# Two hybrid transformer layers on one core: input sums of the MLP made in halves, and two weight sums of the first down projection on GpSimd

## The reference

```python
for l in range(DEPTH):                              # DEPTH = 2
    h = rms_norm(x, norm_mix[l])
    proj = h @ w_in[l]                              # 1024 -> 1792
    ...
    x = x + jnp.concatenate([att, sgu], axis=-1) @ w_o[l]
    h = rms_norm(x, norm_ffn[l])
    x = x + jnp.square(jax.nn.relu(h @ w_up[l])) @ w_down[l]   # 1024 -> 4096 -> 1024
return rms_norm(x, norm_final)
```

## Time and profile before

| | |
|---|---|
| median of 3 executions | 950.86 us (948.45 to 953.03) |
| profiled execution | 949.33 us |
| its span on the core | 947.4 us |
| TensorE matmul busy (PE) | 930.3 us, 98% |
| VectorE busy (DVE) | 707.8 us, 75% |
| ScalarE busy (ACT) | 563.8 us, 60% |
| GpSimd busy (POOL) | 204.8 us, 22% |

### The profile page before, as it was taken

One profiled execution on the slowest core, in us unless ns is written; L12 is line 12 of the kernel. 1 busy time (PEld: TensorE's weight loads), 2 busy tenths in 40 slices (PEclk: granted clock), 3 DMA queues, 4 the chain that ended last, 5 costly groups with the idle time before them and its releaser, 6 DMA issues.

```text
span 947.4 us, 14055 instructions
## 1 busy us (share of the span) xinstructions
PE 930.3 (98%) x5632; PEld 819.0 (86%) x5632; DVE 707.8 (75%) x813; ACT 563.8 (60%) x843; POOL 204.8 (22%) x136
## 2 busy tenths in 40 slices
PE   8999999989999999999999999999899999999997
PEld 5888889978998998899888887899689989989985
DVE  5685525999779869879948752478987897798697
ACT  5556517775576376457655574377645756754764
POOL 2554224110011101011146433240101101101010
PEclk9999999999999999999999999999999999999999
DMA  9442150677668676676543320518668666676772
GB/s 292 127 135 71 42 150 28 167 166 206 147 171 204 134 232 134 178 190 156 165 150 134 112 68 23 155 24 245 139 173 205 149 198 158 161 198 150 205 156 89
DMA packets 40497, 141.76 MB, mean 150 GB/s; under 512 B 5616, under 2 KB 5744, under 8 KB 40432
## 3 DMA queue, kind: packets, MB, share of 16 engines
q1 hardware_dynamic: 28624, 98.32, 30.9%
q0 software_dynamic: 11520, 41.95, 25.3%
q10 hardware_dynamic: 288, 0.59, 0.2%
HBM read 138.74 MB, written 2.10 MB: 149 GB/s over the span
## 4 chain that ended last, share of the span: by engine, by line
PE 89%; DVE 6%; DMA 2%; ACT 1%; issue 1%; POOL 0%; DVEq 0%
PE bank L578 15%; PE bank L579 14%; PE bank L580 14%; PE bank L581 13%; PE bank L583 13%; PE bank L582 13%; DVE wlo L1316 2%; DMA raw<-weights_in 2%; PE bank L605 1%; PE bank L833 1%; PE bank L781 1%; DVE raw L1593 1%; PE bank L816 1%; PE bank L826 1%; PE bank L807 1%
## 5 line engine op out<-in xcount | busy, mean ns | idle before, releaser
L938 ACT ACTIVATE whi<-raw 128x1024 fp32r<-128x1024 f32 x268 | 281.0, 1057 | 165.2 <-PE bank L580 81.2
L1316 DVE TENSOR_TENSOR wlo<-raw,whi 128x1024 fp32r<-128x1024 f32 x218 | 264.8, 1223 | 79.8 <-ACT whi L938 79.4
L581 PE MATMUL bank<-xhi,wlo 128*128 128x256 f32 (+1 forms) x672 | 208.8, 311 | 0.0
L583 PE MATMUL bank<-xlo,whi 128*128 128x256 f32 (+1 forms) x672 | 207.3, 309 | 0.0
L582 PE MATMUL bank<-xhi,whi 128*128 128x256 f32 (+1 forms) x672 | 207.2, 308 | 0.0
L578 PE MATMUL bank<-wlo,fhi 128*128 128x512 f32 x448 | 176.3, 393 | 7.8 <-DVE flo L1580 7.8
L550 POOL DMA_DIRECT2D raw<-weights_in x80 | 69.4, 868 | 509.8 <-DVE raw L1593 236.0
L537 POOL TENSOR_TENSOR wlo<-raw,whi 128x1024 fp32r<-128x1024 f32 x50 | 135.2, 2714 | 195.4 <-ACT whi L938 195.4
L579 PE MATMUL bank<-whi,fhi 128*128 128x512 f32 x448 | 175.8, 392 | 0.0
L580 PE MATMUL bank<-whi,flo 128*128 128x512 f32 x448 | 175.5, 392 | 0.0
L581 PEld LDWEIGHTS bank<-xhi,wlo 128*128 128x128 f32 x672 | 128.3, 191 | 6.8 <-issue 0.3
(11 more groups left out here) (131 smaller groups left out, 1240.7 us busy)
## 6 DMA issues: line engine op xcount, KB each, us to landing
raw<-weights_in SPq DMA_DIRECT2D x172, 512.0 KB, 4.3
raw<-weights_in POOLq DMA_DIRECT2D x80, 512.0 KB, 6.1
xt<-x_in SPq DMA_DIRECT2D x4, 512.0 KB, 8.3
gbc<-gains_in SPq DMA_DIRECT2D x4, 512.0 KB, 4.3
out_t<-xt SPq DMA_DIRECT2D x3, 512.0 KB, 2.6
gbc<-gains_in ACTq DMA_DIRECT2D x1, 512.0 KB, 5.8
bias<-alibi_in SPq DMA_DIRECT2D x2, 256.0 KB, 7.3
wst<-ws_in SPq DMA_DIRECT2D x2, 256.0 KB, 7.0
```

What stands on the lines that cost most here:

```text
L581: pe.matmul(o, wlo[:, s, wc], hi[:, tokens], start=first, stop=False, skip_group_check=on_sum)
L583: return pe.matmul(o, whi[:, s, wc], lo[:, tokens], start=False, stop=last, skip_group_check=on_sum)
L938: act.activation(whi[:, n % SLOTS, :], raw_at(slot), ACT.Copy).then_inc(whi_ready, 1)
L1316: dve.tensor_tensor(wlo[:, n % SLOTS, :], raw_at(raw_slot(n)), whi[:, n % SLOTS, :], ALU.subtract) \
```

## The change

Three edits, all in the MLP of each layer.

1. `xs_make(i)` becomes `xs_make(i, k)`: k = 0 makes the sum for tokens 0 to 127 of each block, k = 1 for the other 128. The halves k = 0 are made inside the norm's last tile, xs_make(0, 0) ahead of its reciprocal and the other three behind its normalisation; the halves k = 1 stand where the whole sums stood. `xs_made` counts eight in place of four, and `xs_high` waits for the half k = 1.
2. In quarter 0, `sum_m6(l, q, g)` for the down projection is done by GpSimd, between its DMAs for M7 and those for M5; VectorE has it no more there.
3. In quarter 0, `make(q, 0)` stands between the low halves of M1's two blocks, one place earlier.

```diff
+def made_x(l, i, k):
+
+    return l * 8 + 4 * k + i + 1
...
+            def sum_m6(l, q, g):
+
+                wait_low(pool, nth(l, group_pos(q, DOWN, M7, g)))
+                pool.wait_ge(raw_landed[PRODUCT_SLOT[DOWN][M1] + g], 16 * block_loads(l, q, DOWN, M1, g))
+                t3 = raw_at(PRODUCT_SLOT[DOWN][M7] + g)
+                pool.tensor_tensor(t3, t3, raw_at(PRODUCT_SLOT[DOWN][M1] + g), ALU.add).then_inc(weights_summed, 1)
...
                     add_blocks(l, q, DOWN, M7)
+                    if q == 0:
+                        sum_m6(l, q, 0)
+                        sum_m6(l, q, 1)
                     add_blocks(l, q, DOWN, M5)
...
+                def xs_make(i, k):
+
+                    x11, x12, x22, x21 = (xf[:, b, :, tok(k)] for b in range(4))
+                    if i == 0:
+                        dve.wait_ge(xf_ready, l * 2 * NT + 6 + 2 * k)
+                        dve.tensor_tensor(s3[:, :, tok(k)], x11, x21, ALU.subtract).then_inc(xs_made, 1)
...
                 for t in range(NT):
                     add(1, t)
                     if t:
                         turned_low(2 * l + 1, t - 1)
+                    if t == NT - 1:
+                        xs_make(0, 0)
                     normed(2 * l + 1, t)
+                for i in range(1, 4):
+                    xs_make(i, 0)
                 turned_low(2 * l + 1, NT - 1)
...
                         low_down(q, M1, 0)
+                        make(q, 0)
                         low_down(q, M1, 1)
...
                     low_down(q, M7, 0)
-                    sum_m6(q, DOWN, 0)
+                    if q:
+                        sum_m6(q, DOWN, 0)
                     factor_low(q, M7)
                     low_down(q, M7, 1)
-                    sum_m6(q, DOWN, 1)
+                    if q:
+                        sum_m6(q, DOWN, 1)
                     low_down(q, M6, 0)
```

More of the change, by code:

```diff
@@ L1139, in xs_high @@
                 def xs_high(i):
-                    made, src = ((1, s3), (3, xf[:, 0, :, :]), (2, xf[:, 3, :, :]), (4, xf[:, 1, :, :]))[i]
-                    act.wait_ge(xs_made, l * 4 + made)
+                    made, src = ((0, s3), (2, xf[:, 0, :, :]), (1, xf[:, 3, :, :]), (3, xf[:, 1, :, :]))[i]
+                    act.wait_ge(xs_made, made_x(l, made, 1))
                     act.copy(factor_x((S3, S2, S5, S4)[i])[0], src).then_inc(xs_hi, 1)
@@ L1514, in add @@
                         .then_inc(x_added, 1)
+                def xs_make(i, k):
[3 more added lines that the diff above has]
+                        dve.tensor_tensor(s3[:, :, tok(k)], x11, x21, ALU.subtract).then_inc(xs_made, 1)
+                    elif i == 1:
+                        dve.wait_ge(xs_made, made_x(l, 0, k))
+                        dve.tensor_tensor(x21, x22, x21, ALU.subtract).then_inc(xs_made, 1)
+                    elif i == 2:
+                        dve.wait_ge(xs_made, made_x(l, 1, k))
+                        dve.scalar_tensor_tensor(x11, x21, -1.0, x11, ALU.mult, ALU.subtract).then_inc(xs_made, 1)
+                    else:
+                        dve.wait_ge(xs_made, made_x(l, 2, k))
+                        dve.scalar_tensor_tensor(x12, x11, -1.0, x12, ALU.mult, ALU.subtract).then_inc(xs_made, 1)
                 for t in range(NT):
@@ L1621, in _ @@
                     if q == 0:
-                        xs_make(0)
+                        xs_make(0, 1)
                         low_up(q, M7, 0)
@@ L1626, in _ @@
                         low_up(q, M7, 1)
-                        xs_make(1)
-                        xs_make(2)
+                        xs_make(1, 1)
+                        xs_make(2, 1)
                         low_up(q, M6, 0)
@@ L1640, in _ @@
                         low_up(q, M5, 0)
-                        xs_make(3)
+                        xs_make(3, 1)
                         up_sum(q, M4, 0)
@@ L1677, in _ @@
                         up_sum(q, M5, 1)
-                    make(q, 0)
+                        make(q, 0)
                     low_down(q, M7, 0)
-                    sum_m6(q, DOWN, 0)
+                    if q:
+                        sum_m6(q, DOWN, 0)
                     factor_low(q, M7)
                     low_down(q, M7, 1)
-                    sum_m6(q, DOWN, 1)
+                    if q:
+                        sum_m6(q, DOWN, 1)
                     low_down(q, M6, 0)
```

## The result

| | before | after |
|---|---|---|
| median | 951.05 us (6 executions, 948.45 to 953.03) | 963.28 us (6 executions, 961.85 to 965.96) |
| ratio | | 1.0129, 95% interval 1.0109 to 1.0149 |
| span of the profiled execution | 947.4 us | 961.3 us |

The change makes the kernel 12.2 us slower. The forecast was 956.4 us, which is 5.5 us slower, and a range to 963.0. The sign was right, the loss is more than twice the forecast, and the time is just outside the range. The two profiled executions lie 13.9 us apart; the one before took 949.33 us, 1.7 under its median.

The account below looks back on a forecast made before the run. TensorE, busy 98% of the span, was taken as the bound. A layer: +1.0 - 0.25 + 2.0 = +2.75, two layers +5.5 us, on the median 950.86 giving 956.4; range 952.5 to 963.

Parts of the forecast that it names:

- The prices that were taken from held instructions in the mixer: Earlier rows: held VectorE multiplies end 0.55 us (128x512) or 1.09 us (128x1024) after GpSimd; held GpSimd 2.26 after VectorE.
- I take it that VectorE wins: Norm's last tile: GpSimd asks 0.04 us before the normalisation, yet VectorE goes first; TensorE stands 0.75 us.
- the first rival: GpSimd wins at the norm's last tile, TensorE stands 3.0 us; 960.4 us, 964 with slow clock; chance 0.28.
- The row that I leaned on: VectorE's second multiply began within 0.01 us of GpSimd's 51.74; GpSimd was held, 2.94 us.
- The forecast's term of +1.0 us a layer: Norm to M6's second up low half: late VectorE makes TensorE 1.0 us later than before.
- +2.0 - 0.25 a layer: Quarter 0 down projection: M6's factor 2.0 us later through holding by GpSimd's sums, less 0.25 from the fourth sum.
- The late half of the fourth sum: At 184.75, saves between nothing and 0.54 us of what follows; 0.25 taken.
- The moved make: make(q, 0) moves into VectorE's 0.94 us of idleness in quarter 0's down projection and costs nothing.
- M4's adding DMA: Quarter 0 down: issued behind GpSimd's sum 2, its low half ends by 220.4, TensorE wants it at 221.7; covered by 1.3 us.
- if the wait at M6 shrinks: Sign that the forecast is wrong; it expected TensorE's waits at M6 about 1.3 us longer each.
- four rows of holding, not five: The prediction cited five rows all showing holding against its third rival, that GpSimd's sum doesn't hold VectorE, chance 0.10.

Follow-up runs that it names:

- e5: Kernel before plus a VectorE subtraction with two SBUF inputs (128x512) ahead of the norm's last reciprocal; 957.56 us, 1.0072 of the kernel before.
- e6: Kernel before plus a VectorE reduction with one SBUF input, same place and columns; 951.14 us, 1.0004 of the kernel before.
- e2: Kernel before with only the quarter 0 weight sums for M6 moved to GpSimd; 956.63 us, 1.0056 of the kernel before.
- e7: e2 with three GpSimd zero fills in place of each add, M6 left out of both quarter 0 down projections; 952.95 us, 1.0017 of the kernel before.
- e4: Changed kernel plus one small ScalarE square root in the norm's last tile, so GpSimd asks later; 958.29 us, 1.0079 of the kernel before.
- e3: Kernel before with only make(q, 0) moved one place earlier in quarter 0; 950.39 us, 0.9994 of the kernel before.
- e1: Kernel before with only the halved input sums; 957.18 us, 1.0059 of the kernel before.
- e10: Kernel before with, in quarter 0, make 0 earlier, both hidden(M5) before M1's second copy, M6's factor before its second block's low half; 946.39 us, 0.9958.

## Why the prediction was right or wrong

**Right: the mechanism and the sign.** VectorE and GpSimd hold each other up when VectorE's instruction has two SBUF inputs and GpSimd's reads SBUF. e5 against e6 shows the first condition, e2 against e7 the second. The prices that were taken from held instructions in the mixer came out within 0.05 us: the first half 1.61 (1.64 by the sum, 157.76 to 159.40), M7's factor 2.64 (2.66), make 1 3.39 (3.43), the second sum 3.28 (3.32).

**Wrong: the step "I take it that VectorE wins".** GpSimd won in both layers, by 0.01 us in the first (159.43 to 159.44) and 0.04 in the second. That was the first rival, with 0.28 against 0.40 for the forecast. The row that I leaned on has both starting at 51.74 us. It tells nothing of a case in which GpSimd is ahead, and my own times had it ahead, by 0.04 us. The forecast's term of +1.0 us a layer became +2.8, as the rival's 3.0 had it. When GpSimd is made to ask later (e4), the term is +0.96. So the arithmetic of both branches held, and the choice between them failed.

**Wrong: the clock left out at that place.** It fell in one of the two layers, 2.7 us more, and the forecast's sum had no term for it. The rival's text had it, at 1.8 us for each layer, and the range ended below it. With both branches joined, 9.5 + 1.8 to 2.7, the first rival gives 962.2 to 963.1, and the measured 963.28 is that case. That it comes within a microsecond is partly luck, since what the clock takes differs between executions (last section).

**Right: the down projection.** The forecast was +2.0 - 0.25 a layer; measured +3.16 and +1.25. Most of the scatter is the load of M1's second block, which is issued when VectorE has made the low half of M5's second, and which VectorE's chain waits for. Before, in the first layer, the end of that low half and the start of ScalarE's copy of the loaded block were 187.71 and 195.97, 8.26 us apart:

```profile
186.49 1.22 DVE L1316 TENSOR_TENSOR wlo<-raw,whi 128x1024 fp32r<-128x1024 f32 x1
195.97 1.06 ACT L938 ACTIVATE whi<-raw 128x1024 fp32r<-128x1024 f32 x1 [2.17 <-DMA raw<-weights_in]
```

In the changed kernel 190.16 and 199.91, 9.75 us:

```profile
188.93 1.23 DVE L1331 TENSOR_TENSOR wlo<-raw,whi 128x1024 fp32r<-128x1024 f32 x1 [0.19 <-ACT whi L953]
199.91 1.06 ACT L953 ACTIVATE whi<-raw 128x1024 fp32r<-128x1024 f32 x1 [3.42 <-DMA raw<-weights_in]
```

In the second layer the same stretch is 8.81 and 8.32 us. Taking out these differences, +1.5 and -0.5, leaves +1.7 in either layer, against 1.75. What is left splits as the sum had it. From the copy to M6's factor it is 17.09 and 17.15 us against 15.15 and 15.16, so +1.9 and +2.0 for a forecast of +2.0. In e2 and e3, with nothing changed ahead of it, the load took 10.78 and 9.46 us in the first layer: in kernels that are alike up to it, it scatters by over 2 us. I had read it once and taken it as fixed.

**Partly right: the edges.** The late half of the fourth sum was given 0.25 us. From M6's second low half to M5's second it is 10.36 us in both layers of the changed kernel and 10.63 and 10.62 before, 0.26 us less; of the other 0.28 (0.54 was the most it could save) 0.19 is a wait for ScalarE's copy, in the row at 188.93. That is the middle value that was taken. The moved make costs and brings nothing, as forecast (e3). M4's adding DMA was called covered, by 1.3 us. It isn't quite: TensorE waits 0.53 and 0.35 us at M4, though for VectorE's adds behind a late low half, and this is most of the last row of the table above. The sign "if the wait at M6 shrinks" was a bad one: it shrank in the first layer, to 2.92 us, while the factor came later, because the clock had fallen behind the wait at M7. And the earlier trace rows has four rows of holding, not five; the fifth is GpSimd's 2.79 us in the earlier trace rows.

**The chances.** 0.63 for slower by over 0.5% was on the right side. The range should have held the first rival with its clock fall, 964, since one with 0.28 may not be cut in half.

## What to carry to other kernels

Before an instruction is put into another engine's idle time, look at what GpSimd does then: a VectorE instruction with two SBUF inputs next to a GpSimd one that reads SBUF waits for it whole, and so does what stands behind it. The trace books this as busy time, so compare durations of the same form and not waits. Work moved to GpSimd is not taken off VectorE if VectorE has two-input work at that moment. And when two requests fall within 0.1 us of each other, neither the forecast nor its range may rest on one outcome.

## What the runs showed of the hardware that I had not expected

- **Which of the two goes first is settled within hundredths of a microsecond**, and by who asked first as the starts show it: GpSimd 0.01 us ahead wins (159.43 against 159.44), VectorE 0.05 ahead wins (e4). In each kernel looked at for this, the order was the same in both layers.
- **A wait of 2.7 us is followed by a lower clock in some layers and not in others**: 0.50 in the second layer after and 1.00 in the first, 0.57 in the first layer of e1 and 1.00 in the second, though the waits are equal to 0.02 us. In e10 a wait of 2.53 us was followed by 0.60 and one of 2.12 by 1.00, but the changed kernel's 2.24 us at M7 was followed by 0.65 and e4's 2.56 us by 1.00. So between 2.24 and 2.75 us either can follow. What decides it is open; no run here separates it.
- **One fall of the clock doesn't have one price.** Behind the same wait at M6 (3.64 to 3.66 us) the granted clock lost TensorE 1.7 us in both layers before and 3.1 and 2.9 us in e3 (estimates from windows of 1 us). In e3 it had already fallen while TensorE was idle, and stayed at 0.50 longer after the restart. e3's profiled execution took 952.0 us against a median of 950.39. Differences of 1 to 2 us are to be read from many executions and not from one trace.
- **A 512 KB load on the path scattered between 8.3 and 10.8 us** from its release to the copy, in the same place of the first layer in kernels that differ only behind it (before, e2, e3, e7, e10). In the down projection it explains most of the difference between the layers of the changed kernel (1.9 us apart, 2.0 by the load).
